# A fused two-layer denoising step: step 0 of the expert loop taken out of the loop and run on one sample, the most picked experts first

## The reference, cut to what matters

```
g_idx  = argmax(h @ rg_w + rg_b)                 # 1 of 4 groups
top_i  = top_k(e_logits of that group, 2)        # 2 of its 8 experts
hid    = silu(h @ w_gate[e]) * (h @ w_up[e])     # 1024 -> 256, for each picked expert
out    = sum_e gate_e * (hid @ w_down[e])        # 256 -> 1024
```

## Time and profile before

| | us |
|---|---|
| median of 3 runs | 944.24 |
| lowest, highest | 942.35, 951.48 |
| profiled execution, its own time | 949.07 |
| its span, first to last instruction | 947.3 |
| PE busy | 851.7 (90%) |
| DVE busy | 492.3 (52%) |
| ACT busy | 195.8 (21%) |

### The profile page before, as it was taken

One profiled execution on the slowest core, in us unless ns is written; L12 is line 12 of the kernel. 1 busy time (PEld: TensorE's weight loads), 2 busy tenths in 40 slices (PEclk: granted clock), 3 DMA queues, 4 the chain that ended last, 5 costly groups with the idle time before them and its releaser, 6 DMA issues. The chain is left out here.

```text
span 947.3 us, 14602 instructions
## 1 busy us (share of the span) xinstructions
PE 851.7 (90%) x5328; PEld 523.9 (55%) x5328; DVE 492.3 (52%) x1287; ACT 195.8 (21%) x546; POOL 42.0 (4%) x62
## 2 busy tenths in 40 slices
PE   3899989999999989988899969799889987999993
PEld 1687865777677766573344436344555652544351
DVE  1244689888864674775234326011265771532256
ACT  0125632222211311120011102001462210110110
POOL 1000230000010000000000001000000000000000
PEclk9999999999999989999899979999979998999997
DMA  9931279564454510099989772843200599989961
GB/s 366 417 166 67 89 277 396 206 237 182 181 193 168 202 50 15 18 422 420 401 329 425 285 325 66 349 151 144 104 1 1 213 421 420 378 346 404 423 277 44
DMA packets 29070, 226.85 MB, mean 239 GB/s; under 512 B 4104, under 2 KB 4520, under 8 KB 8032
## 3 DMA queue, kind: packets, MB, share of 16 engines
q1 hardware_dynamic: 25504, 214.57, 56.3%
q0 software_dynamic: 3520, 11.66, 3.7%
HBM read 286.74 MB, written 2.39 MB: 305 GB/s over the span
## 5 line engine op out<-in xcount | busy, mean ns | idle before, releaser
L1267 PE MATMUL ps<-arena 128*32 128x512 f32 x960 | 115.9, 632 | 26.1 <-DMA arena<-in_w_exp 24.0
L1452 ACT ACTIVATE arena<-ps 128x256 f32<-128x256 f32 (+1 forms) x122 | 47.9, 429 | 229.6 <-PE ps L830 135.1
L1267 PEld LDWEIGHTS ps<-arena 128*32 128x32 f32 x960 | 31.6, 115 | 106.8 <-issue 74.6
L1321 PE MATMUL ps<-arena 128*128 128x512 f32 x192 | 84.8, 601 | 5.8 <-issue 5.0
L914 PE MATMUL ps<-arena 128*128 128x256 f32 x368 | 81.6, 380 | 1.9 <-ACT arena L1460 1.9
L914 PEld LDWEIGHTS ps<-arena 128*128 128x128 f32 x368 | 69.0, 189 | 14.5 <-ACT arena L1460 2.1
L1232 PEld LDWEIGHTS ps<-arena 128*128 128x128 f32 x544 | 63.0, 193 | 17.8 <-issue 10.9
L830 PE MATMUL ps<-arena 128*128 128x128 f32 x432 | 62.3, 281 | 9.8 <-DVE arena L2510 4.7
L1232 PE MATMUL ps<-arena 128*128 128x128 f32 x544 | 66.6, 280 | 4.4 <-DVE arena L2326 4.4
L1021 PE MATMUL ps<-arena 128*128 128x192 f32 x320 | 64.5, 348 | 4.8 <-DVE arena L2052 2.4
L2420 DVE TENSOR_SCALAR arena<-arena 128x256 f32<-128x256 f32 x15 | 4.4, 296 | 120.5 <-ACT arena L1669 120.0
(11 more groups left out here) (340 smaller groups left out, 1113.9 us busy)
## 6 DMA issues: line engine op xcount, KB each, us to landing
arena<-in_w_exp SPq DMA_DIRECT2D x180, 1024.0 KB
arena<-in_mod_w SPq DMA_DIRECT2D x24, 2048.0 KB, 7.7
arena<-in_od_in_w SPq DMA_DIRECT2D x6, 2048.0 KB, 11.4
arena<-in_ev_in_w SPq DMA_DIRECT2D x5, 2048.0 KB, 28.7
arena<-in_ev_out_w SPq DMA_DIRECT2D x2, 2048.0 KB, 7.4
arena<-gate_rows POOLq DMA_DIRECT2D x8, 512.0 KB, 6.3
arena<-in_ln POOLq DMA_DIRECT2D x4, 1024.0 KB, 11.0
arena<-in_od_out_w SPq DMA_DIRECT2D x2, 2048.0 KB, 7.9
```

The lines of the kernel that those rows point to most:

```text
L1267: mm = pe.matmul(ps[32 * c:32 * c + 32, 6, :], xg[:, k, 32 * c:32 * c + 32], EW[:, c, k * 512:(k + 1) * 512], start=(k == 0), stop=(k == K ...
L1321: mm = pe.matmul(BK.bank(key), hT[:, k, s * T:(s + 1) * T], slot(("odin", c))[:, k, :], start=(k == 0), stop=(k == KT - 1))
L1452: BK.drained_by(A(out, take(key)[:, 0:n], ACT.Copy), key)
```

## The change

Four edits in one.

```diff
-                for a2 in range(2):
-                    BK.wait_drained(pe, ("LT", u, j, a2))
-                    key = ("LT", u, j + 1, a2)
-                    BK.wait_free(pe, key)
-                    for i in (2 * a2, 2 * a2 + 1):
-                        mm = pe.matmul(BK.bank(key)[:, (i % 2) * P:(i % 2 + 1) * P], now[:, i, 0:P], lt[i],
-                                       start=True, stop=True)
-                    mm.then_inc(filled, 1)
+                BK.wait_drained(pe, ("LT", u, j, 1))
+                key = ("LT", u, j + 1)
+                BK.wait_free(pe, key)
+                for i in range(4):
+                    mm = pe.matmul(BK.bank(key)[early, i * HD:(i + 1) * HD], now[:, i, early], lt[i][:, late],
+                                   start=True, stop=True)
+                mm.then_inc(filled, 1)
...
                 for h in range(2):
-                    sp.wait_ge(S(f"gu{h}_done{l}"), it + 1)
+                    sp.wait_ge(S(f"gu{h}_done{l}"), it)
                     for c in range(NC):
                         load(f"gu{h}", *GU[h], c, expert[c], cond=fresh[c])
-                sp.wait_ge(S(f"down{l}"), it * 2 + 2)
+                sp.wait_ge(S(f"down{l}"), it * 2)
                 for c in range(NC):
                     load("down", *DN, c, expert[c], cond=fresh[c])
             if l == 0:
+                sp.wait_ge(S("summed"), 2 * NS)
+                load_chunk(sp, FIRST_OF_1 + 1)
+                load_chunk(sp, FIRST_OF_1 + 2)
                 sp.wait_ge(S("x_new"), norm_no(0, 1, 1) + 1)
...
+            BK.wait_drained(pe, ("g0", l, 1))
+            pe.wait_ge(S(f"gu0_loaded{l}"), 64)
+            gate_up(xg, 0)
+            side_free("tot")
+            pe.wait_ge(S("nchunks"), l + 1)
...
+            pe.wait_ge(S(f"gu1_loaded{l}"), 64)
+            for k in range(4, KT):
+                gate_up(xg, k)
...
+            BK2.wait_drained(pe, ("eid", l))
+            pe.wait_ge(S(f"gates{l}"), 1)
+            turn(0)
+            down(0)
...
-                own.link(TS(col(34), bank[0:32, 0:1], 0.0, 1e6, ALU.is_equal, ALU.mult))
-                read(STT(col(35), bank[0:32, 0:1], 32.0, col(34), ALU.mult, ALU.add), "first")
-                own.link(TT(col(35), col(35), cst[0:32, C_COL:C_COL + 1], ALU.add))
+                own.inc(TS(col(39), bank[0:32, 0:1], float(CH), None, ALU.min))
+                read(STT(col(35), bank[0:32, 0:1], -32.0, cst[0:32, C_COL:C_COL + 1], ALU.mult, ALU.add), "first")
...
+            own.link(STT(col(34), col(33), sc[0:32, 48:49], col(37), ALU.min, ALU.mult))
...
+            hidden(0)
+            gathered(1)
...
+            own.link(TT(by_step(kept, NC), per_col(eid[:, 0:NC], 1), by_step(eid[:, NC:], NC), ALU.subtract))
+            own.link(TT(kept, kept, held, ALU.mult))
+            own.link(TT(eid[:, NC:], eid[:, NC:], kept, ALU.add))
...
+            gates(0, 3, place)
+            step_end(0)
```

More of the change, by code:

```diff
@@ L343, in build, with halves_of @@
     LEVELS = 7
+    def halves_of(z):
+        first, second = slice(0, P // 2), slice(P // 2, P)
+        return (first, second) if z == 0 else (second, first)
     STEPS = ["gram", "rhs"] + list(range(LEVELS)) + ["out"]
@@ L445, in plan_moe @@
             BK.add(("xT", f"e{l}", 1, h2), "act" if h2 == 0 else "dve")
+        BK.add(("pos0", l), "dve")
         BK.add(("lg", l, 1), "dve")
+        for h2 in range(2):
+            BK.add(("g0", l, h2), "act")
         for h2 in range(2):
@@ L692, in _ @@
                 sp.dma_start(CV, a["cache_v"]).then_inc(S("ld_cache"), 16)
-                for i in range(FIRST_OF_1 + 1, len(chunks)):
+                for i in range(FIRST_OF_1 + 3, len(chunks)):
                     load_chunk(sp, i)
@@ L1029, in wkv_level @@
                     mm = pe.matmul(BK.bank(key)[:, i * HD:(i + 1) * HD], lt[i], now[:, i, P:P + HD], start=True, stop=True)
+                mm.then_inc(filled, 1)
+            else:
+                BK.wait_drained(pe, ("LT", u, j))
+                key = ("X", u, j)
+                BK.wait_free(pe, key)
+                for i in range(4):
+                    mm = pe.matmul(BK.bank(key)[late, i * HD:(i + 1) * HD], LT[early, q, j % 2, i, 0:HD],
+                                   now[early, i, P:P + HD], start=True, stop=True)
                 mm.then_inc(filled, 1)
@@ new lines, in moe @@
+            pe.wait_ge(S(f"gates{l}"), 1)
+            turn(0)
+            down(0)
+            pe.wait_ge(S("cleared"), 4 * l + 4)
+            pe.wait_ge(S(f"meta{l}"), 1)
+            steps = pe.value_load(meta[0:1, 0, 0:1], min_val=MINS, max_val=MAXT)
+            with pe.Fori(1, steps) as n:
+                pe.wait_ge(S(f"xg_act{l}"), n)
+                pe.wait_ge(S(f"xg_dve{l}"), n)
+                for h in range(2):
+                    pe.wait_ge(S(f"gu{h}_loaded{l}"), n * 64 + 64)
+                    for k in range(4 * h, 4 * h + 4):
+                        gate_up(xg, k)
+                pe.wait_ge(S(f"y_read{l}"), n)
+                pe.wait_ge(S(f"y_read_dve{l}"), n)
+                gather(n + 1)
+                pe.wait_ge(S(f"gates{l}"), n + 1)
+                pe.wait_ge(S(f"tG{l}"), n)
+                turn(n)
@@ L2139, in wkv_level @@
                                  now[:, :, P:P + HD], ALU.add), key)
+            else:
+                key, late = ("X", u, j), halves_of(UNITS[u][1])[1]
+                BK.drained_by(TT(now[late, :, P:P + HD], take(key)[late, 0:256].rearrange("p (i n) -> p i n", i=4),
+                                 now[late, :, P:P + HD], ALU.add), key)
         def finals(z):
@@ L2380, in moe @@
-            own.link(STT(more, slot_of, float(CH), both(D_), ALU.is_lt, ALU.mult))
-            own.link(STT(slot_of, both(start), float(CH), slot_of, ALU.mult, ALU.add))
-            own.link(TT(slot_of, slot_of, more, ALU.add))
-            for pick, oh in ((0, P1), (1, P2)):
-                own.link(TT(rv(R_T, 64), oh, rv(R_SL, 64), ALU.mult))
-                own.link(V.tensor_reduce(sc[:, 42 + 2 * pick:44 + 2 * pick], rv(R_T, 64, "p (s n) -> p s n", s=NS), AX, ALU.add))
-            at, chunk, col = sc[:, 42:46], sc[:, 6:10], sc[:, 10:14]
@@ new lines, in moe @@
+            later = rv(R_SL, 64, "p (s n) -> p s n", s=NS)
+            pos = take(("pos", l))[:, 0:64].rearrange("p (s n) -> p s n", s=NS)
+            read(TT(later, pos, both(rv(R_TK, 32)), ALU.subtract), "pos")
+            side_read(TS(sc[:, 40:41], side("tot")[:, 0:1], 1.0 / NC, None, ALU.mult), "tot")
+            own.link(TS(rv(R_KV, MAXS), upto(MAXS), sc[:, 40:41], None, ALU.is_lt))
+            own.link(V.tensor_reduce(total, rv(R_KV, MAXS), AX, ALU.add))
+            own.link(STT(col(34), col(33), sc[0:32, 48:49], col(37), ALU.min, ALU.mult))
@@ new lines, in moe @@
+            own.link(STT(delta, delta, sc[:, 49:50], rv(R_B1, 32), ALU.add, ALU.subtract))
+            own.link(TT(beyond, beyond, both(delta), ALU.mult))
+            own.link(TT(later, moved, beyond, ALU.add))
+            own.inc(TT(rv(R_T, 64), P1, rv(R_SL, 64), ALU.mult))
+            own.link(TT(rv(R_T4, 64), P2, rv(R_SL, 64), ALU.mult))
+            for pick, v in enumerate((R_T, R_T4)):
+                own.inc(V.tensor_reduce(sc[:, 42 + 2 * pick:44 + 2 * pick], rv(v, 64, "p (s n) -> p s n", s=NS), AX, ALU.add))
@@ new lines, in moe @@
+            own.wait()
+            at, chunk, column, lin = sc[:, 42:46], sc[:, 6:10], sc[:, 10:14], rv(R_LIN, 4)
+            over = lambda v, n: v.rearrange("p (t o) -> p t o", o=1).broadcast_to([P, 4, n])
+            under = lambda v, n: v.rearrange("p (o c) -> p o c", o=1).broadcast_to([P, 4, n])
+            ge4, ge3 = rv(R_GE, 16, "p (t c) -> p t c", t=4), rv(R_GE, 12, "p (t c) -> p t c", t=4)
+            own.link(TS(chunk, at, 1.0 / CH, 0.5 / CH - 0.5, ALU.mult, ALU.add))
+            own.link(TS(chunk, chunk, float(3 * 2 ** 22), None, ALU.add))
@@ L2435, in sum_half @@
+            steps = dve.value_load(meta[0:1, 0, 0:1], min_val=MINS, max_val=MAXT)
+            with dve.Fori(1, steps) as n:
+                hidden(n)
+                gathered(n + 1)
+                step_end(n)
             def sum_half(s, half):
```

408 lines of the change are left out of this document (218 added, 190 removed).

## The result

The changed kernel takes 965.72 us (median of 4 runs, 963.49 to 967.06), the kernel before 945.12 (4 runs beside it): ratio 1.0193, 95% interval [1.0162, 1.0225]. A later repeat gave 964.02 (6 runs) against 947.98, 1.0174 [1.0131, 1.0217]. Both intervals exclude no change. Over all runs of this study the medians are 965.1 (10 runs) and 946.9 (80 runs): +18.3. The forecast was +9.9 and 954: the sign was right, the size about half.

What follows compares the result with a forecast made beforehand. PE was taken to bound the recurrence, PE (18.1 us a step) and weight loads alternately the expert loops. +2 + 20 - 6.6 - 5.5 = +9.9 gave 959.0 against the profiled execution, 954 against the median; range 943 to 966.

Steps and rivals of the forecast that it cites:

- bunched loads behind a hole in the flow: Expert loops: weight flow stops after step 0's weights, 17 us in layer 0 and 34 in layer 1; loads pile up late.
- the recurrence: Recurrence term: 0.87 us saved a unit, 7 for eight if PE bounds all of it; taken as -5.5 us.
- layer 0: Layer 0's expert loop: early waits go, steps 4 to 6 wait for weights; end 574.5 against 572.60, +2 us.
- Layer 1, +20: Layer 1's expert loop: steps 5 to 7 wait for weights, 29.9 us apart; last scatter 947.6 against 928.82, taken as +20.
- 1.4 as a correction: Layer 1 term: the same reckoning over the loads of before ended 1.4 us too early, so +20 was taken.
- Rival A: Expert loops: the bytes decide; six parts fewer give -15 us, with the other two edits -27: 917; chance 0.08.
- Step 0, +0.5 a layer: Peeled step 0: half 1 waits for weights, then DVE is late; step 1 starts at 445.2 against 444.68, +0.5 us.
- steps 1 to 3 need 0, 2, 2 and keep to 18.1: Layer 0's loop: columns with a new expert in steps 1 to 3, each step at PE's 18.1 us; step 4 due at 499.5.
- Early chunks, -6.6: Layer 1's input projection: chunks asked at 576.3 land before PE wants them; 5.02 us wait and 1.6 of low clock go.
- 0.48 for eight: Recurrence: eight passes with 64 columns of weights and 64 moving columns, at 0.06 us each, take 0.48 us.
- lower bound, 2.5 if VectorE is soon the later one: Recurrence: eight units give only 2.5 us if DVE, busy 0.74 on average there, is soon the later engine.
- a granted clock of 0.62 "halfway": After a weight wait in the loops: granted clock 0.62, read as halfway between 1.2 and 2.4 GHz; PE slower there.

Runs made afterwards that it cites:

- Experiment 1: Changed kernel, but step 0 takes the experts of ranks 2, 4, 1 and 6 instead of 0 to 3, spreading the same number of loads: 942.33 us.
- experiment 2: Changed kernel without the weight loads after step 0 of layer 1 (stale weights, only its time is used): 931.42 us.
- Experiment 3: Changed kernel with the gate scalars and gate rows of step 0 made ahead of the hidden values on VectorE: 952.60 us.
- Experiment 9: Changed kernel with GpSimd's three transfers of each loop asked after the down products of step 0 instead of step 1: 962.21 us.
- experiment 5: Changed kernel with all chunks of layer 1's input projection asked after the last norm again, as in the kernel before: 971.45 us.
- experiment 6: Kernel before with only the corner powers of the recurrence and the two early chunks added, no peeled step, old choice of experts: 941.33 us.
- experiment 4: Changed kernel with the recurrence of before (full last power and last level, two ScalarE copies): 969.23 us.
- Experiment 10: Both kernels unchanged, profiled and timed again: the kernel before 946.87 us, the changed kernel 964.02 us.
- experiments 1 to 7: Follow-up runs of variants of the changed kernel or of the kernel before, timed beside the kernel before; medians of the variants from 931.42 to 971.45 us.

## Why the prediction was right and wrong

The direction and the mechanism of the loss (bunched loads behind a hole in the flow) were right, the size was not: +9.9 forecast, +20.6 measured (+18.3 over all runs). The steps that failed are the recurrence (-5.5 forecast, about -2.5 measured), layer 0 (+2 forecast, +3.8 measured), and that nothing in the sum stood for the scatter of single executions (6.2 of the first 20.6; this part is attributed by comparing runs, not isolated).

- **Layer 1, +20: right in sum, +20.3, and in part by luck.** From the start of step 1 to the last scatter 159.1 us were forecast and 159.1 measured, 18.2 more than before (787.88 to 928.82). The forecast had then added 1.4 as a correction, which was not needed; but step 1 starts 2.1 later after the signal than before, not 0.5, and the two errors cancel. The start of step 1 in the profile (788.5 forecast, 784.15) is earlier because everything ahead of it is. The empty flow from 777 to 811, the waits in steps 5, 6 and 7 and their distance of 29.9 all came as written. Experiment 1 shows the cause (same bytes, spread: 142.3), experiment 2 the price of all of it (32.3 over a loop without loads). Rival A, that the bytes decide, is refuted by the result itself (six parts fewer, and slower) and by experiment 1 (the same bytes, 17 us less). The Trainium skill's rule ("DMA: Bandwidth & Descriptors", section "Where 436 GB/s comes from": loads from HBM are bound at about 358 GB/s a core, a stack's 716 divided by its two cores) would have given 965, which is what the runs took; yet the end of layer 1 ran at 422 GB/s with one core at work, and its 159.1 us are those of 2.49 us a part. The sum by the rule hit the time for a reason that the trace contradicts.
- **Step 0, +0.5 a layer: right in layer 0, +0.7** (signal to step 1: 47.6 for 46.9), **too small in layer 1, +2.1** (48.6 for 46.5). Half 1 waits for weights, and VectorE's queue holds the transposes, as written. Experiment 3 shows that this was an order, not a necessity, and that it cost 4.6 us in layer 0 and 5.2 in layer 1. The prediction had priced it without asking which instruction could go into the idle time.
- **Layer 0, +2: too small, +3.8.** The failed step is "steps 1 to 3 need 0, 2, 2 and keep to 18.1": step 3 waited 1.1 and 1.3. The sum had left out GpSimd's transfers, which take the flow's time just then. Experiment 9 shows that with them out of the way the three steps do keep to 18.1, and that this is worth only 0.4 to 0.8 us of the 1.8, since the later steps wait for the same bytes. The rest was not isolated, and it is no more than the scatter of this loop: before's code took 172.5 to 177.1 in three profiles.
- **Early chunks, -6.6: right**, -7.6 between the two traces, 7.2 in experiment 5 (4.7 in experiment 6, where a wait of 2.37 stood elsewhere); no idle before the group that stood 5.02 in the earlier trace rows.
- **Recurrence, -5.5: failed, about -2.5.** The rows of one unit after the change (L1022 the corner of the last power, L1046 the level on the late half, L1039 the level before it):

```profile
253.38 0.68 PE L1022 MATMUL ps<-arena 128*64 128x64 f32 x8
253.99 1.10 PE L1039 MATMUL ps<-arena 128*128 128x64 f32 x8
257.92 0.68 PE L1046 MATMUL ps<-arena 64*64 64x64 f32 x8
258.53 1.10 PE L1066 MATMUL ps<-arena 128*128 128x64 f32 x8
```

  The failed step is "0.48 for eight" passes. The corner takes 0.61 (253.38 to 253.99), with half of the array's columns, and the half level 0.61 too (257.92 to 258.53), with a quarter of the array: the price of 0.06 a pass, taken from a row where the passes follow each other in pairs, does not hold for eight. L1039 grew from 0.84 to 0.94 (253.99 to 254.93). A unit thus saves 0.38 + 0.23 - 0.10 = 0.5, not 0.87; eight units 4, of which 2.5 to 2.6 arrive at equal clock (experiment 4; the signal itself is 2.0 earlier). The prediction's lower bound, 2.5 if VectorE is soon the later one, gave the right number from prices that were too high; that VectorE, busy 0.74 of the time, holds the missing 1.5 was argued, and no run isolates it.
- **The executions.** The profiles differ by 14.4 where the forecast had 9.9: 3.5 of it in the recurrence with the planning behind it, 1.8 in layer 0, 0.3 in layer 1, less 1.0 in the chunks. The other 6.2 up to the 20.6 of the first comparison are the positions of single executions in their spread: the profile of before was 2.2 over its median of 80 runs, that median is 1.8 over the 4 runs first compared; the profile of the change was 1.6 under its median of 10, and that is 0.6 under the first 4. Experiment 10 shows where such microseconds can lie: in stretches of equal code at another granted clock. A sum of rows from one execution has no term for this; that the change itself runs more often at the low clock in its other executions is not excluded.
- **A reading of the rows.** The prediction calls a granted clock of 0.62 "halfway" between the two levels. The lower level is 0.5 of full speed, so 0.62 is a quarter of the way. No term of the sum hangs on it.

## What to carry to other kernels

A busy share of a transfer queue does not tell what a change that moves demand is worth: list what each step must load and when its buffer falls free, and look for steps that ask nothing before steps that ask everything. A choice of work that saves loads early and piles them up late can cost more than one that saves nothing. When a step is taken out of a loop to start early, write down what the shared engine (here VectorE) does in every gap, because a wait removed in front of it returns as the next engine's wait, as the plan's did here when only the gates were moved. And compare a stretch in two traces only where the granted clock is the same: over the recurrence, equal code differed by as much as the edit was worth.

## What was not expected of the hardware

- Eight passes of 64 rows by 64 columns took as long (0.61 us, 0.076 each) as eight of 128 rows with 64 columns of weights (0.61): here half of the rows saved nothing. Eight with 128 columns of weights and as many moving columns (64) took 0.84 in before (252.91 to 253.75).
- The same code differs between executions by 8 us, 6 of them in and around the recurrence, at a granted clock of 0.92 instead of 0.97, where PE idles less (5.7 us of 150) than in the faster one (7.1). Over the 34 runs of before that were timed beside experiments 1 to 7, a mean granted clock lower by 0.01 goes with 6.6 us more.
- The 32 down products behind a wait of 5.19 us for VectorE took 5.64 us, at a granted clock of 0.63; behind one of 1.24 they took 3.64, at 1.00. Cutting 3.95 us of a wait thus brought step 1 forward by 4.6 and 5.2, although 1.6 of a new wait stands before it.
